# Gate builds as one 64-column matmul with the low half added on VectorE, in a two-layer streaming encoder with product-key experts

## The reference

```python
q = (xb @ w_q).reshape(blk, PEER_HEADS, 2, D_HALF)
sc = jnp.einsum('thpd,hpnd->thpn', q, sub_keys)
top_s, top_i = lax.top_k(sc, PEER_TOPK)
cand_s = top_s[:, :, 0, :, None] + top_s[:, :, 1, None, :]
cand_i = top_i[:, :, 0, :, None] * N_KEYS + top_i[:, :, 1, None, :]
best_s, sel = lax.top_k(cand_s.reshape(blk, PEER_HEADS, 256), PEER_TOPK)
idx = jnp.take_along_axis(cand_i.reshape(blk, PEER_HEADS, 256), sel, axis=-1)
gate = jax.nn.softmax(best_s, axis=-1)
act = jax.nn.gelu(jnp.einsum('thkd,td->thk', exp_u[idx], xb))
return jnp.einsum('thk,thkd->td', gate * act, exp_v[idx])
```

## Time and profile before

| | |
|---|---|
| median of 3 runs (lowest, highest) | 3362.18 us (3359.61, 3370.66) |
| the profiled execution's own time | 3359.59 us |
| its span, first to last instruction | 3357.5 us |
| busy: TensorE, VectorE, ScalarE, GpSimd | 89%, 75%, 24%, 30% |
| mean granted TensorE clock | 0.926 of full speed |
| DMA | 1043 MB, mean 311 GB/s |
| expert phases: first build to the last row add | 528 to 1636 us and 2233 us to the end of the span, nearly |

### The profile page before, as it was taken

The page is one execution under the profiler, slowest core; times in us unless marked ns, Lnnn a source line. Parts: engine busy times, 40 slices in busy tenths (PEclk is TensorE's granted clock), DMA queues, the critical chain, the costliest instruction groups (busy, mean ns, idle before and its releaser), DMA issues.

```text
span 3357.5 us, 46623 instructions
## 1 busy us (share of the span) xinstructions
PE 2984.8 (89%) x17310; PEld 2601.9 (77%) x17310; DVE 2511.8 (75%) x5433; ACT 811.2 (24%) x2386; POOL 1019.0 (30%) x840
## 2 busy tenths in 40 slices
PE   6999979999999999767678889789999999998676
PEld 5887868988888888655566857679888888887554
DVE  4277797777777777988643786988777777778787
ACT  3332221211111111111344352222211111111112
POOL 4441022222222222444254411122222222223431
PEclk8899989999999999888878978899999999998787
DMA  4235668999999999999521346679999999999996
GB/s 153 88 104 194 238 262 324 353 389 394 391 394 398 393 392 386 422 421 422 207 81 39 106 163 235 236 270 368 377 391 386 392 398 393 390 370 412 422 421 253
DMA packets 159975, 1043.13 MB, mean 311 GB/s; under 512 B 18480, under 2 KB 23920, under 8 KB 44096
## 3 DMA queue, kind: packets, MB, share of 16 engines
q0 software_dynamic: 92160, 671.13, 50.2%
q1 hardware_dynamic: 63648, 357.59, 28.0%
q10 hardware_dynamic: 4000, 12.36, 1.0%
HBM read 1033.28 MB, written 7.86 MB: 310 GB/s over the span
## 4 chain that ended last, share of the span: by engine, by line
PE 48%; DMA 27%; DVE 14%; issue 8%; ACT 1%; POOL 1%; SPq 0%; DVEq 0%; ACTq 0%; POOLq 0%
DMA gat<-uvg,idxg 23%; PE bank L719 15%; PE bank L732 9%; PE bank L523 7%; DVE acc L1597 6%; PE bank L706 3%; DMA U<-uvg,idxg 3%; PE bank L510 3%; PE bank L511 3%; PE bank L512 3%; DVE gat L1589 2%; PE bank L608 1%; PE bank L540 1%; DVE oneA L1563 1%; DVE B L1569 1%
## 5 line engine op out<-in xcount | busy, mean ns | idle before, releaser
L1273 POOL DMA_INDIRECT gat<-uvg,idxg x580 | 667.8, 1151 | 1842.3 <-DVE acc L1597 1774.7
L732 PE MATMUL bank<-a,V 128*128 128x256 f32 x4096 | 982.0, 401 | 152.1 <-DVE a L1580 152.0
L732 PEld LDWEIGHTS bank<-a,V 128*128 128x128 f32 x4096 | 826.7, 203 | 290.4 <-issue 165.6
L1589 DVE CUSTOM_DVE_ANT_0 gat<-gat,xrow 128x1024 f32<-128x1024 f32 x580 | 708.1, 1221 | 402.1 <-DMA gat<-uvg,idxg 398.1
L719 PE MATMUL bank<-xd,U 128*128 128x256 f32 x4096 | 922.7, 384 | 1.2 <-DMA U<-uvd 1.2
L719 PEld LDWEIGHTS bank<-xd,U 128*128 128x128 f32 x4096 | 778.2, 193 | 103.8 <-DMA U<-uvd 1.6
L1597 DVE SCALAR_TENSOR_TENSOR acc<-gat,wgt,acc 128x1024 f32<-128x1024 f32 x580 | 742.0, 1279 | 28.9 <-ACT wgt L1078 28.7
L1076 ACT ACTIVATE act<-dot 128x1 f32<-128x1 f32 x640 | 129.3, 202 | 1560.2 <-DVE dot L1589 1560.0
L706 PEld LDWEIGHTS bank<-B,oneA 128*128 128x128 f16 x4096 | 282.6, 150 | 18.5 <-DVE oneA L1563 6.3
L706 PE MATMUL bank<-B,oneA 128*128 128x32 f16 x4096 | 284.9, 246 | 5.7 <-DVE oneA L1563 5.3
L523 PE MATMUL bank<-xd,raw 128*128 128x256 f32 x1088 | 248.7, 386 | 7.5 <-DVE xd L1360 7.1
(11 more groups left out here) (195 smaller groups left out, 2462.6 us busy)
## 6 DMA issues: line engine op xcount, KB each, us to landing
U<-uvd SPq DMA_DIRECT2D x128, 1024.0 KB
V<-uvd SPq DMA_DIRECT2D x128, 1024.0 KB
raw<-lin SPq DMA_DIRECT2D x152, 512.0 KB, 3.2
gat<-uvg,idxg POOLq DMA_INDIRECT x580
hsp<-h ACTq DMA_DIRECT2D x2, 2304.0 KB, 13.8
hx<-hsp SPq DMA_DIRECT2D x2, 2304.0 KB, 16.7
sk_g<-skT ACTq DMA_DIRECT2D x2, 1024.0 KB, 4.9
sk_d<-skT ACTq DMA_DIRECT2D x2, 1024.0 KB, 8.3
```

Source lines behind the costliest of these rows:

```text
L732: mm = pe.matmul(bank[b][:, TD * (d % 2):TD * (d % 2) + TD], V[:, s, o:o + P], a[:, s, TD * k:TD * k + TD], start=(first and k == 0 and d ...
L1273: pool.indirect_dma_start(row(l, s), None, uvg[l], bass.IndirectOffsetOnAxis(idxg[:, s:s + 1], 0)).then_inc(g_in[k], 16)
L1589: dve.tensor_tensor_reduce(u, u, xrow[:, min(s // P, 2), :], 1.0, 0.0, ALU.mult, ALU.add, dot[:, s % 8:s % 8 + 1]).then_inc(dot_done, 1)
```

## The change

1. A build is 16 matmuls instead of 32. High and low part are the two halves of one moving operand of 64 columns. A bank then has room for 8 of the 16 tokens, so each build fills both banks. ScalarE copies the high halves to `Wr` (two instructions), and VectorE adds the low halves to it (`add_low`, two instructions, one operand in PSUM), which frees the banks. The lead is 18 builds. Both parts stay multiplied by GS, and the last add of the layer takes 1/GS in.
2. The scores before the first build end one pair earlier, and one stands between build 0 and build 1. On ScalarE the weights of "hot0" stand behind the first of the remaining GELUs instead of the last.
3. The masks of `choose` and what goes with them have the head as their innermost dimension, so that no operand is broadcast along the innermost one.

```diff
-LEAD = PER + 1
+LEAD = PER + 2
...
+        def gate_half(l, m, u):
+            cols = slice(TG * u, TG * u + TG)
+            high, low = (bank[2 + u][:, :].rearrange("p (t a j e) -> p a j e t", t=TG, a=2, e=2)[:, k] for k in range(2))
+            return gate_block(m // PER, m % PER)[:, :, :, cols], high, low
...
-                pe.wait_ge(free[2 + s], m // 2 + BASE[f"bld{l}"][2 + s])
-                for t in range(TB):
-                    for part in range(2):
-                        mm = pe.matmul(bank[2 + s][:, CHUNK * t:CHUNK * (t + 1)], oneA[:, s, t // TG, :, t % TG],
-                                       B[:, s, part, :, t], start=(t == 0 and part == 0), stop=True,
-                                       skip_group_check=True)
-                mm.then_inc(full[2 + s], 1)
+                for u in range(TB // TG):
+                    pe.wait_ge(free[2 + u], BASE[f"bld{l}"][2 + u] + m)
+                    for t in range(TG):
+                        mm = pe.matmul(bank[2 + u][:, 2 * CHUNK * t:2 * CHUNK * (t + 1)], oneA[:, s, u, :, t],
+                                       B[:, s, :, :, TG * u + t], start=(t == 0), stop=True, skip_group_check=True)
+                    mm.then_inc(full[2 + u], 1)
...
-                for i in range(n, RING0):
+                for i in range(n, RING0 - 1):
                     expert_scores(l, i, i % 2)
                 for m in range(LEAD):
                     build(l, m, m % 2)
-                    if m >= 1:
-                        expert_scores(l, RING0 + m - 1, (m + 1) % 2)
+                    if RING0 - 1 + m < RING:
+                        expert_scores(l, RING0 - 1 + m, (m + 1) % 2)
...
-                if c >= 1:
+                if m >= PER:
                     act.wait_ge(a_done, NPAIR * l + m - PER + 1)
-                act.activation(gate_block(c, m % PER), bank[b][:, :].rearrange("p (t j e) -> p j e t", t=TB, e=2),
-                               ACT.Copy, scale=1.0 / GS).then_inc(free[b], 1)
+                for u in range(TB // TG):
+                    w, high_, _ = gate_half(l, m, u)
+                    act.wait_ge(full[2 + u], BASE[f"bld{l}"][2 + u] + m + 1)
+                    act.activation(w, high_, ACT.Copy).then_inc(w_high, 1)
...
-                for i in range(n, RING0):
+                gelu(l, n)
+                weights_at(l, "hot0")
+                for i in range(n + 1, RING0 - 1):
                     gelu(l, i)
-                for m in range(LEAD):
+                for m in range(1, LEAD):
                     weights_at(l, f"hot{m}")
-                    if m >= 1:
-                        to_w(l, m - 1)
-                    if m >= 2:
+                    to_w(l, m - 1)
+                    if RING0 + m - 1 < RING:
                         gelu(l, RING0 + m - 2)
...
-                                  d1[0:n, c, :, :, None].rearrange("p q j o -> p j q o").broadcast_to([n, TOPK, PH, TOPK]),
+                                  d1[0:n, c, :, None, :].broadcast_to([n, TOPK, TOPK, PH]),
                                   ALU.mult).then_inc(prod_done, 1)
...
-                dve.wait_ge(full[2 + s], BASE[f"bld{l}"][2 + s] + m // 2)
+                if m >= 2:
+                    dve.wait_ge(full[3], BASE[f"bld{l}"][3] + m - 1)
...
+            def add_low(l, m):
+                for u in range(TB // TG):
+                    w, _, low = gate_half(l, m, u)
+                    dve.wait_ge(w_high, 2 * (NBLD * l + m) + u + 1)
+                    dve.tensor_tensor(w, w, low, ALU.add).then_inc(free[2 + u], 1)
...
                 for m in range(LEAD):
+                    if m == LEAD - 1:
+                        gate_product(l, 0)
                     one_hot(l, m)
                     steps_at(l, f"hot{m}")
-                gate_product(l, 0)
+                    if m >= 1:
+                        add_low(l, m - 1)
                 for i in range(NPAIR):
+                    if 1 <= i <= NBLD - LEAD + 1:
+                        add_low(l, i + LEAD - 2)
                     if i + LEAD < NBLD:
                         one_hot(l, i + LEAD)
...
-                    dve.tensor_tensor(h[:, dt, 0:TD], hx[:, dt, 0:TD], bank[4 + dt // 2][:, TD * (dt % 2):TD * (dt % 2) + TD],
-                                      ALU.add)
+                    dve.scalar_tensor_tensor(out=h[:, dt, 0:TD],
+                                             in0=bank[4 + dt // 2][:, TD * (dt % 2):TD * (dt % 2) + TD],
+                                             scalar=1.0 / GS, in1=hx[:, dt, 0:TD], op0=ALU.mult, op1=ALU.add)
```

More of the change, by code:

```diff
@@ L655, in second_rank @@
                 pe.wait_ge(free[6], BASE[f"rk{l}_{i}"][6])
-                pe.matmul(bank[6][0:n, 0:P], scaled[0:n, 0, 0:n], bph[0:n].rearrange("p q k -> p (q k)"),
+                pe.matmul(bank[6][0:n, 0:P], scaled[0:n, 0, 0:n], bph[0:n].rearrange("p k q -> p (k q)"),
                           start=True, stop=False)
@@ L659, in second_rank @@
                     gap = 2 + GAPS.index(STARTS[j] - STARTS[j - 1])
-                    mm = pe.matmul(bank[6][0:n, 0:P], scaled[0:n, gap, 0:n], mask[0:n, j, :, :].rearrange("p q k -> p (q k)"), start=False,
+                    mm = pe.matmul(bank[6][0:n, 0:P], scaled[0:n, gap, 0:n], mask[0:n, j, :, :].rearrange("p k q -> p (k q)"), start=False,
                                    stop=(j == TOPK - 1))
@@ L673, in gathered_index @@
                             width = (heads.stop - heads.start) * TOPK
-                            mm = pe.matmul(bank[7][rows, 0:width], scaled[0:n, 1 - a_, 0:n], prod[0:n, a_, j, heads, :].rearrange("p q k -> p (q k)"),
+                            mm = pe.matmul(bank[7][rows, 0:width], scaled[0:n, 1 - a_, 0:n], prod[0:n, a_, j, :, heads],
                                            start=(a_ == 0 and j == 0), stop=(a_ == 1 and j == TOPK - 1),
@@ L1494, in choose @@
                         dve.wait_ge(full[4 + last % 2], BASE[f"gt{l}"][4 + last % 2] + 1)
-                dve.tensor_tensor(mask[0:n], bph[0:n, None, :, :].broadcast_to([n, TOPK, PH, TOPK]),
-                                  ranks[0:n, 0, :, None, :].broadcast_to([n, TOPK, PH, TOPK]),
+                dve.tensor_tensor(mask[0:n], bph[0:n, None, :, :].broadcast_to([n, TOPK, TOPK, PH]),
+                                  ranks[0:n, 0, :, None, 0:PH].broadcast_to([n, TOPK, TOPK, PH]),
                                   ALU.is_ge).then_inc(mask_done, 1)
@@ L1512, in choose @@
                 link(dve.reciprocal(rs[0:n], sm[0:n]))
-                dve.tensor_tensor(gt[0:n], ex[0:n], rs[0:n, :, None].broadcast_to([n, PH, TOPK]),
+                dve.tensor_tensor(gt[0:n].rearrange("p k q -> p q k"), ex[0:n], rs[0:n, :, None].broadcast_to([n, PH, TOPK]),
                                   ALU.mult).then_inc(gate_done, 1)
                 dve.wait_ge(full[6], BASE[f"rk{l}_{i}"][6] + 1)
-                dve.tensor_copy(rank2[0:n].rearrange("p q k -> p (q k)"), bank[6][0:n, 0:P]).then_inc(free[6], 1)
+                dve.tensor_copy(rank2[0:n].rearrange("p k q -> p (k q)"), bank[6][0:n, 0:P]).then_inc(free[6], 1)
                 dve.wait_ge(free[6], BASE[f"rk{l}_{i}"][6] + 1)
                 dve.wait_ge(prod_done, 2 * (NTC * l + i) + 1)
-                dve.tensor_tensor(mask[0:n], rank2[0:n, None, :, :].broadcast_to([n, TOPK, PH, TOPK]),
-                                  ranks[0:n, 1, :, None, :].broadcast_to([n, TOPK, PH, TOPK]),
+                dve.tensor_tensor(mask[0:n], rank2[0:n, None, :, :].broadcast_to([n, TOPK, TOPK, PH]),
+                                  ranks[0:n, 1, :, None, 0:PH].broadcast_to([n, TOPK, TOPK, PH]),
                                   ALU.is_equal).then_inc(mask_done, 1)
@@ L1523, in choose @@
                 dve.tensor_tensor(prod[0:n, 1], mask[0:n],
[L1524 removed]
+                                  t2[0:n, c, :, None, :].broadcast_to([n, TOPK, TOPK, PH]),
                                   ALU.mult).then_inc(prod_done, 1)
@@ L1576, in gate_product @@
                 for b in (2, 3):
-                    dve.wait_ge(free[b], BASE[f"bld{l}"][b] + TD // TB // 2 * (i // PER + 1))
+                    dve.wait_ge(free[b], BASE[f"bld{l}"][b] + TD // TB * (i // PER + 1))
                 if i >= 2:
```

39 lines of the change are left out of this document (19 added, 20 removed).

## The result

The kernel after takes 3373.2 us (median of 20 executions, 3363.3 to 3382.1), the kernel before 3361.8 (20, 3351.4 to 3371.1): 1.0038 times as long, 95% interval 1.0028 to 1.0048. The forecast was 3367, with a sum of +6.4; the two profiled executions differ by 3369.0 - 3357.5 = 11.5 us.

What follows compares the result with a forecast made beforehand. The prediction took VectorE's gather loop, not TensorE, to set the pace. Its terms, -10.6 + 0 + 13 + 5 - 1 = +6.4 on 3359.6, gave 3366.0 (3368.6 by the median), stated as 3367, range 3332 to 3408.

Steps and rivals of the forecast that it cites:

- What bounds the kernel: Whole expert phase: the change is worth what it does to the gather loop, not to TensorE.
- The builds: TensorE's builds: 16 matmuls at 64 ns, 1.02 us saved each; nothing saved if the moving side counted fully (2.05 us).
- The adds: VectorE's two adds per build: 0.68 us, a quarter exposed in the middle, +13 us over both layers.
- the other estimate, 0.78: Two adds of a build by the Trainium skill's formula: 0.78 us, making terms that hold adds 15% larger.
- The tail: Adds of each layer's last seven builds: hidden behind the DMA, +0; if not, +10 us.
- The lock-step and pair 40: Builds wait for VectorE's previous add; stalls of about 7 us before U gathers: +5 us layer 0, -1 layer 1.
- The first builds: Lead-ins: VectorE's slot 2 at 524.4 instead of 537.3, then 8.6 us slots; -10.6 us layer 0, 0 layer 1.
- The rank masks: Expert choices: 21 us less VectorE work, none on the path; 0, at best -10 us.
- The exposed adds at three quarters: Rival in the gather loop: adds three quarters exposed, +40 us middle, +10 lead-in, 3406 by the median; chance 0.25 with milder forms.
- TensorE as the bound: Rival: a pair takes 14.95 us, -1.0 us for each of 40 x 2, down to about 3270; chance 0.12.
- The adds hidden altogether: Rival: adds cost nothing, lead-in slots of 8.3 us, -17 us, 3345 by the median; chance 0.20.
- the slower clock: Rival: TensorE's new waits slow its clock, 0.3 us a pair, +24 us, 3390; chance 0.08.

Runs made afterwards that it cites:

- both_dense: Kernel after with the build matmuls' moving and stationary columns both read side by side (gates wrong, same work): 3338.3 us, 0.9923 of the kernel before.
- old_builds_dense_iota: Kernel before with new first-build order, masks, later first gather into U, operands as token pairs, and the compares' constant stored as pairs: 3318.9 us, 0.9862.
- moving_dense: Kernel after with only the build matmuls' 64 moving columns read side by side (gates wrong, same work): 3346.9 us in one execution.
- no_adds: Kernel after without VectorE's adds of the low halves, ScalarE's copies freeing the banks: 3349.9 us, 0.9959 of the kernel before.
- first_late_u: Kernel before with new first-build order and masks, and the first gather into U four steps later; no 64-column builds or adds: 3352.0 us, 0.9959.

## Why the prediction came out as it did

**What bounds the kernel: right in direction, too absolute.** VectorE's gather loop sets the pace of the middle: with 172 us less TensorE work the middles shortened by 9 and 4 us of some 640. But TensorE's time was not worthless, as some 22% of what is taken from it reaches the end, through the lead-ins (15 us by the trace of both_dense, 20 by that of old_builds_dense_iota) and less through the middles (13 and 5 us).

**The builds: wrong.** "I take the weight load as the price and 64 ns for 64 columns too" failed; 120 ns were measured, the other bound that the step named. The saving was 0.12 us a build, and TensorE's pair is 15.77 us instead of 14.90. Mis-sized with it: TensorE's wait ahead of a build, forecast as about 1 us each, is 56.5 us in all, 0.44 each, because TensorE is busy for longer: in both_dense, where a build takes 0.59 us, it is 143.2 us, 1.1 each.

**The adds: the price right, what reaches the end too low.** 0.66 us a build (522.53 to 523.19) for 0.68; the other estimate, 0.78, was too high. The forecast had +13 for the adds and +4 for the stall that the banks bring, 17 of 87 us; the runs show 27 (20 to 33) for adds and banks together. In the lead-in they cost nothing, as said. The tail, put at nothing, is +3.6 and +1.3 us in the table: there VectorE's slots with an add stand at 12.8 us for 12.2 (3070.71 - 3057.86, 3059.93 - 3047.68), with no wait in them that the add could hide in. Between kernels with and without adds the tails differ by 1.4 us a layer in the mean, so this is a small term and not well measured.

**The lock-step and pair 40: right.** "At 8.8 us both layers would stand about 7": the release comes 10.2 and 11.4 us after the slot's start, of which 0.9 is the dearer build, and VectorE stands 7.7 and 9.1 us. At the end of pair 40 this had cost 8.9 us in both layers; the forecast took off "what the DMA catches up", and with pair 41 the table has +3.6 and -0.4 us, 3.2 in sum for a forecast of +4. Moving the first gather into U took back 17 us (10 to 25), more than these 3.2, since it also removed the stall that the kernel before has in layer 1.

**The first builds: right for slot 2 (523.2 for 524.4), off for the slots behind it.** They last 8.9 us, locked to TensorE's 1.93 + 6.93, instead of 8.6, so layer 0 gains 6.6 us and not 10.6. That is the step on the builds again. (The terms written out for slot 2 add up to 524.2, not 524.4.)

**The rank masks: right,** 0 by their own run (5 us either way). ScalarE's second copy: nothing found that it costs, though no run tests it alone.

**The time was met in part by luck.** The sum rested on builds at 64 ns, and moving_dense is nearly that kernel (59 ns): it took 3346.9 in its one execution, 20 us under the forecast and below the kernel before. So two errors offset each other: builds that cost 120 ns instead of 64, and a working in which TensorE's time behind the lead-ins was worth nothing. With the builds that it assumed, the same working would have missed the sign.

**The rivals.** The exposed adds at three quarters are not what these 95 us did, but of 123 us of VectorE time on top of them 70% reached the end: the slack runs out. TensorE as the bound would have given 80 us for 1 us a pair, and 1.34 us gave 39 us. The adds hidden altogether fall with no_adds, and with them the reading that some 4 us of queueing in each gather would hide them entirely. The granted clock stayed (0.925 for 0.926; 0.99 for 1.00 from 700 to 1300 us), so the slower clock falls. Its example, the group of 9.89 us in the earlier trace rows, was at the lower level for its first part only: 0.50 up to 1341 us, 1.00 from 1345 on.

## What to carry to other kernels

Fewer, wider matmuls saved almost nothing here, as each streamed strided operands: look at how far apart the moving and stationary elements lie before counting instructions; a layout in pairs of f16 made 2.05 us into 0.82 without cost to VectorE, once the constant that it compares with was packed the same way. Waits of 300 us for DMA on an engine are no budget for new work: of the adds' 95 us 28% reached the end, of 123 us more on top of them 70%, and of 119 us in a kernel without adds half. A gather is issued only when the engine has come round (GpSimd's gathers waited 1787 us in all for VectorE's row adds). Where a queue in program order waits for another engine's last instruction of a phase, shifting it by a few steps is a change of one number, and was worth 17 us in the kernel after and nothing measurable in first_late_u, where VectorE did not stall there.

## What the runs showed of the hardware that was not expected

- A build matmul of 128 stationary columns, f16, start to start: 120 ns with 64 moving columns 32 bytes apart, 59 ns with them dense and the stationary ones still 16 bytes apart, 37 ns with both dense or both 4 bytes apart; with 32 moving columns 64 ns at 32 bytes (stationary 16 bytes apart), 25 ns with both 4 bytes apart.
- A compare of 128x1024 f16 on VectorE went from 684 to 1065 ns when one operand was read as 2 of every 8 elements, of 128x512 from 418 to 612 ns; with that operand dense as pairs, though broadcast over the groups of tokens, 704 and 418 (the kernel before has 701 and 418).
- A product of 128x2048 f16 with one operand broadcast along its innermost dimension took 2292 ns, without that 1224.
